# Expert units loaded in two halves, the input half released by the up step

## The reference, cut to what matters

```python
def block(tb):                                   # 128 tokens
    s = jnp.einsum('thsk,hsnk->thsn', qr, sub_keys)
    top_s, top_i = lax.top_k(s, PEER_TOPK)
    ...
    gate = jax.nn.softmax(best_s, axis=-1)       # 8 heads x 16 experts a token
    act = gelu(jnp.einsum('td,thkd->thk', tb, expert_u[idx]))
    w = gate * act
    return jnp.einsum('thk,thkd->td', w, expert_v[idx])
```

## Time and profile before

| | |
|---|---|
| median of 3 runs | 3339.25 us (3337.97 to 3349.36) |
| the profiled execution, its own time | 3346.74 us |
| its span in the profile | 3344.9 us |
| TensorE busy, share of the span | 2946.0 us, 88% |
| VectorE busy | 2258.0 us, 68% |
| ScalarE busy | 1341.0 us, 40% |
| GpSimd busy | 202.2 us, 6% |
| moved by transfers | 645.03 MB, 193 GB/s on average |
| expert stage of layer 0 | about 965 to 2040 us of the span |
| expert stage of layer 1 | about 2635 to 3313 us of the span |

### The profile page before, as it was taken

How to read it: one execution, slowest core, us unless ns; L and a number is a source line. 1 busy time by engine, 2 the same in 40 slices (tenths; PEclk the granted TensorE clock), 3 DMA queues, 4 the chain that set the end, 5 groups by cost and what they waited for, 6 DMA issues and landing times.

```text
span 3344.9 us, 48195 instructions
## 1 busy us (share of the span) xinstructions
PE 2946.0 (88%) x17119; PEld 2417.9 (72%) x17119; DVE 2258.0 (68%) x4420; ACT 1341.0 (40%) x2255; POOL 202.2 (6%) x238
## 2 busy tenths in 40 slices
PE   6999899754789999999999998978772899999998
PEld 2855454543679898898999996767662788888886
DVE  1337241669987777777777774275459988888886
ACT  2122220211974444444444443122213855655553
POOL 0000000000001111111111110000000000000000
PEclk7899999866999999999999998989996999999998
DMA  9122212524237877878777773223230378777774
GB/s 373 58 83 79 85 38 88 203 87 177 109 142 255 285 265 275 271 267 281 255 253 254 251 251 113 76 95 114 98 139 26 116 298 299 303 300 287 292 287 188
DMA packets 127609, 645.03 MB, mean 193 GB/s; under 512 B 11520, under 2 KB 45472, under 8 KB 55584
## 3 DMA queue, kind: packets, MB, share of 16 engines
q1 hardware_dynamic: 98656, 434.13, 35.7%
q0 software_dynamic: 28864, 209.76, 17.5%
HBM read 624.02 MB, written 19.79 MB: 192 GB/s over the span
## 4 chain that ended last, share of the span: by engine, by line
PE 66%; DVE 16%; DMA 8%; ACT 7%; issue 3%; DVEq 0%; ACTq 0%; SPq 0%
PE ps L611 65%; DMA ring<-in_experts 6%; ACT hot L1336 2%; DMA ring<-in_w_mod 1%; DVE hot L1827 1%; DVE gbuf L1850 1%; ACT ehi L1349 1%; DVE topi L1744 1%; DVE topi L1752 1%; DVE hot L1822 1%; DVE sc L1746 1%; ACT gateB L1322 1%; DVE top L1741 1%; DVE top L1749 1%; DVE hot L1825 0%
## 5 line engine op out<-in xcount | busy, mean ns | idle before, releaser
L611 PE MATMUL ps<-h2a,ehi 128*128 128x384 f32 x2048 | 522.4, 336 | 3.5 <-DVE elo L1837 3.5
L1837 DVE TENSOR_TENSOR elo<-ring,ehi 128x1024 fp32r<-128x1024 f32 x256 | 312.3, 1221 | 125.0 <-ACT ehi L1349 124.6
L611 PEld LDWEIGHTS ps<-h2a,ehi 128*128 128x128 f32 x2048 | 372.8, 188 | 15.2 <-DVE elo L1837 5.2
L1349 ACT ACTIVATE ehi<-ring 128x1024 fp32r<-128x1024 f32 x256 | 270.6, 1058 | 259.8 <-DMA ring<-in_experts 259.5
L1872 DVE TENSOR_TENSOR elo<-ring,ehi 128x1024 fp32r<-128x1024 f32 x256 | 312.9, 1222 | 68.0 <-ACT ehi L1375 67.9
L1375 ACT ACTIVATE ehi<-ring 128x1024 fp32r<-128x1024 f32 x256 | 269.9, 1054 | 205.9 <-PE ps L611 205.4
L611 PE MATMUL ps<-h2b,ehi 128*128 128x192 f32 x2048 | 349.1, 274 | 2.1 <-DVE elo L1837 2.1
L611 PE MATMUL ps<-h2a,elo 128*128 128x384 f32 x1024 | 343.7, 336 | 0.0
L611 PEld LDWEIGHTS ps<-h2b,ehi 128*128 128x128 f32 x2048 | 320.8, 192 | 23.9 <-DVE elo L1837 6.6
L611 PE MATMUL ps<-hT,ring 128*128 128x512 f32 (+1 forms) x896 | 307.7, 502 | 0.0
L594 POOL DMA_INDIRECT gbuf<-in_expert_rows,gidx x192 | 185.5, 966 | 1834.8 <-DVE yg L1860 1700.0
(11 more groups left out here) (320 smaller groups left out, 4556.4 us busy)
## 6 DMA issues: line engine op xcount, KB each, us to landing
ring<-in_experts SPq DMA_DIRECT2D x256, 1024.0 KB, 4.8
ring<-in_w_mod SPq DMA_DIRECT2D x48, 1024.0 KB, 7.7
ring<-in_w_side SPq DMA_DIRECT2D x24, 1024.0 KB, 4.9
ring<-in_w_front SPq DMA_DIRECT2D x12, 1024.0 KB, 4.9
ring<-in_w_merge SPq DMA_DIRECT2D x16, 768.0 KB, 4.3
ring<-in_w_q SPq DMA_DIRECT2D x12, 1024.0 KB, 5.0
gate_scratch<-spill SPq DMA_DIRECT2D x48, 256.0 KB, 2.0
gateA<-gate_scratch SPq DMA_DIRECT2D x4, 3072.0 KB, 20.3
```

Source lines behind the costliest of these rows:

```text
L611: return pe.matmul(out, w, x, start=start, stop=stop, **k)
L1349: act.activation(ehi[:, k % 2, :], ring[:, (u + k) % RING, 0:DM], ACT.Copy).then_inc(uhi_ready, 1)
L1837: v.tensor_tensor(elo[:, r, 0:DM], ring[:, r, 0:DM], ehi[:, k % 2, :].bitcast(F32), ALU.subtract).then_inc(ulo_ready, 1)
```

## The change

Every expert unit is loaded by two transfers of 512 KB: columns 0 to 1023 by `load_in`, columns 1024 to 2047 by `load_out`. `load_in` of unit n waits for `a_ready` of up(n-4), `load_out` of unit n for `used` of down(n-4). The halves have semaphores of their own: `u_in` (new) for the input half, for which `u_high` now waits, and `unit_in` for the output half, for which `v_high` now waits besides `used`. On the queue the input half of unit n+1 stands ahead of the output half of unit n. The rest of the kernel stays. Without its file names and blank lines:

```diff
@@ -354,6 +354,7 @@
         const_in = sem("const_in")
         unit_in = [sem(f"unit_in{s}") for s in range(RING)]
+        u_in = [sem(f"u_in{s}") for s in range(RING)]
         keys_in = sem("keys_in")
         mcst_in = sem("mcst_in")
@@ -477,6 +478,48 @@
                     for k in range(RING):
                         load(u + head + k, src[bass.ds(i * RING + (head + k), 1)].rearrange("o p n -> (o p) n"), i, RING)
+            def load_in(l, k, i=None):
+                e, n = BASE[("experts", l, 0)] + k, units_before(("experts", l, 0)) + k - RING
+                if i is not None:
+                    sp.wait_ge(a_ready, i * RING + (n + 1))
+                    src = a["experts"][l, bass.ds(i * RING + k, 1)].rearrange("o p n -> (o p) n")
+                else:
+                    if k >= RING:
+                        sp.wait_ge(a_ready, n + 1)
+                    else:
+                        sp.wait_ge(used[e % RING], e // RING)
+                    src = a["experts"][l, k]
+                sp.dma_start(ring[:, e % RING, 0:DM], src[:, 0:DM]).then_inc(u_in[e % RING], 16)
+            def load_out(l, k, i=None):
+                e = BASE[("experts", l, 0)] + k
+                sp.wait_ge(used[e % RING], e // RING if i is None else i + e // RING)
+                src = a["experts"][l, k] if i is None else a["experts"][l, bass.ds(i * RING + k, 1)].rearrange("o p n -> (o p) n")
+                sp.dma_start(ring[:, e % RING, DM:2 * DM], src[:, DM:2 * DM]).then_inc(unit_in[e % RING], 16)
+            def experts_begin(l):
+                for k in range(RING):
+                    load_in(l, k)
+                for k in range(RING):
+                    load_out(l, k)
+            def experts_turns(l, first, n):
+                with sp.Fori(0, n) as i:
+                    for k in range(RING):
+                        load_in(l, first + k + 1, i)
+                        load_out(l, first + k, i)
+            def experts_end(l):
+                for k in range(NK - RING, NK):
+                    if k + 1 < NK:
+                        load_in(l, k + 1)
+                    load_out(l, k)
             for st in stages:
                 kind, l, h = st
                 u = BASE[st]
@@ -528,9 +571,8 @@
                     if half is not None:
                         stream(u + WQ_UNITS, a["w_mod"][l + 1, MOD_UNITS // 2 * half:MOD_UNITS // 2 * (half + 1)], MOD_UNITS // 2)
                 elif kind == "gates" and l < DEPTH - 1:
-                    gb, e = groups_before(st), BASE[("experts", l, 0)]
-                    for k in range(RING):
-                        load(e + k, a["experts"][l, k])
+                    gb = groups_before(st)
+                    experts_begin(l)
                     with sp.Fori(0, dense_tokens(l) // 16) as i:
                         for b in range(2):
@@ -540,24 +582,22 @@
                 elif kind == "experts" and l < DEPTH - 1:
                     back = a["gate_scratch"].rearrange("m p n t -> p m n t")
-                    def turns(first, n):
-                        with sp.Fori(0, n) as i:
-                            for k in range(RING):
-                                load(u + first + k, a["experts"][l, bass.ds(i * RING + (first + k), 1)].rearrange(
-                                    "o p n -> (o p) n"), i, RING)
+                    load_in(l, RING)
                     for b in range(NEAR // BACK):
-                        turns(RING + BACK * b, BACK // RING)
+                        experts_turns(l, RING + BACK * b, BACK // RING)
                         s_ = slice(BACK * b, BACK * (b + 1))
                         for parity in range(2):
                             sp.wait_ge(spill_out[parity], 8 * spills_before(st))
                         count(sp, w_ready, units_before(st) + BACK * (b + 1))
                         sp.dma_start(gateA[:, :, s_, :], back[:, :, s_, :]).then_inc(gate_back, 16)
-                    turns(RING + NEAR, (NK - NEAR) // RING - 1)
+                    experts_turns(l, RING + NEAR, (NK - NEAR) // RING - 2)
+                    experts_end(l)
                 elif kind == "experts":
-                    stream(u, a["experts"][l], NK)
+                    experts_begin(l)
+                    load_in(l, RING)
+                    experts_turns(l, RING, NK // RING - 2)
+                    experts_end(l)
                 elif kind == "final":
                     sp.wait_ge(fin_ready, KD)
                     sp.dma_start(a["out"], fout[:, :, :]).then_inc(stored, 16)
@@ -1343,7 +1383,7 @@
                     actT = peer_tiles(l)[3]
                     def u_high(k, i):
-                        arrived(act, u + k, i, RING)
+                        act.wait_ge(u_in[(u + k) % RING], i * 16 + 16 * ((ub + k) // RING + 1))
                         if k >= 2 or not isinstance(i, int):
                             act.wait_ge(a_ready, i * RING + (ub + k - 1))
                         act.activation(ehi[:, k % 2, :], ring[:, (u + k) % RING, 0:DM], ACT.Copy).then_inc(uhi_ready, 1)
@@ -1371,6 +1411,7 @@
                     def step(k, i, ahead):
+                        arrived(act, u + k, i, RING)
                         unit_used(act, u + k - 2, i, RING)
                         act.activation(ehi[:, 2 + k % 2, :], ring[:, (u + k) % RING, DM:2 * DM], ACT.Copy
                                        ).then_inc(vhi_ready, 1)
```

## The result

| | before | changed |
|---|---|---|
| median, runs side by side on one chip | 3342.99 us (3337.97 to 3349.36, 4 runs) | 3298.4 us (3297.42 to 3302.09, 4 runs) |
| ratio of the two | 1 | 0.9863, interval 0.9849 to 0.9877 |
| span of the profiled execution | 3344.9 us | 3295.6 us |
| expert stage of layer 0, first up step to last down step | 1071.3 us | 1063.7 us |
| expert stage of layer 1, likewise | 677.7 us | 638.9 us |

The change makes the kernel 44.6 us faster by the medians. The prediction said 44, and 3295 us for the median, from a median of before that lay 3.7 us lower (3339.25 against 3342.99). The last two lines are from the starts and ends of the matmuls in the traces. The stages give 38.8 and 7.6 us; the other 2.9 us of the spans' difference lie outside them, where nothing was changed.

What follows compares the result with a forecast made beforehand. TensorE's matmuls were taken as the bound, with stalls in layer 1 from late expert loads. 37 us (layer 1) plus 7 us (layer 0) make 44; 3339.25 less 44 gives 3295 us, range 3290 to 3303.

Steps and rivals of the forecast that it cites:

- Step 1: Layer 1's expert stage: input halves asked for earlier end ScalarE's waits and TensorE's stalls; 37 us won, between 20 and 41.
- The clock's part: Layer 1's expert stage: the granted clock drops to 0.50 behind long stalls; 6 us taken as won back.
- the prediction's 33.0 us: Layer 1's expert stage: TensorE's weight loads waited 26.4 us for wB and 6.6 us for elo, the most to win there.
- The 3 us kept for the edge: Layer 1, edge of each four-unit turn: the vector engine's margin is thin, about 0.6 us, so 3 us of stalls stay.
- The first rival: Turn's edge takes over: vector engine or gathered row 1.2 us later at 31 edges, 19 us lost, 3314 us; chance 0.09.
- Steps 2 and 3: Expert stages: ScalarE's later wait for the output half, and 512 loads instead of 256 on the sync queue, each cost nothing.
- Step 4: Layer 0, four gate returns: less data ahead lands unit 20's input half 2.3 us sooner; 7 us won, between 3 and 8.4.
- The rule about sizes: Expert loads: at least 1 MiB per DMA is asked for; halves in series would add some 180 us over 128 units.
- Loads not the cause: Expert stage: stalls aren't the loads', or halves don't come sooner; 0 to 10 us won, 3329 to 3339; chance 0.07.
- transfers the bound: Layer 1's expert stage: smaller transfers carry only 280 GB/s where 308 are needed, 22 us more there, 3354 us; chance 0.05.

Runs made afterwards that it cites:

- series of releases: Four half-transfer kernels with the input half released at down n-4, up n-3, down n-5, up n-4 (the change): 3329.44, 3310.57, 3296.51, 3298.4 us.
- halves alone: Against the changed kernel, the input half is released with the whole unit's event, down step of unit n-4, output half right behind it: 3329.44 us, ratio 0.9967.
- the wide product: Changed kernel plus an unread 128x1024 vector-engine product, without a wait of its own, at each of 31 turn edges in layer 1: 3318.32 us, ratio 0.9915.
- quarters: Against the changed kernel, each half is loaded in two transfers of 256 KB, four a unit: 3298.77 us, ratio 0.9839.
- The run that makes the prediction's mechanism true: Against the changed kernel, the queue order puts unit 20's input half behind the return of gates in layer 0: 3303.72 us, ratio 0.9856.

## Why the prediction was right, and where it wasn't

**Step 1, layer 1: right in mechanism and size.** 37 us were forecast (39 to 41, less 3 kept), 38.8 measured, close to the 39 by waits and clock. What the forecast needed was a landing within 10.6 us; the halves land in 4.0 to 7.3 us, median 5.4, not quite the 4 to 6 given. The series of releases shows the cause: the loss falls with the release, at one and the same size. The prediction had not seen that halves alone, without any earlier release, win 22 us of it; this is worth knowing, since it means that the gain isn't one thing.

The clock's part can be estimated from the traces. The kernel before was at the lower level of 1.2 GHz in four stretches of this stage, each right behind a long stall: the two of the earlier trace rows and, with length, busy PE, granted clock, DMA share and GB/s,

```profile
3193.00:3196.00 3.00, 3.00 (x9) 0.51 0.01 5
3238.00:3240.50 2.50, 2.50 (x11) 0.50 0.14 16
```

The four are some 14 us together. At half speed they give back about 7 us, an estimate, where 6 were forecast; in the changed kernel the granted clock is 1.00 over the stage. TensorE's own idle time was 24.4 us. The rest of the 38.8 us, between 7 and 8, shows neither as idle time nor as clock. The run with the wide product has such a part too: 18.0 us lost at a clock of 1.00, of which TensorE stood idle for 11.0. So the prediction's 33.0 us, the waits of the weight loads, was the right row to add up, and TensorE's idle time would have been too little.

**The 3 us kept for the edge: wrong, nothing is lost there.** The margin was put at 0.57 to 0.76 us. Measured with extra products it is 0.5 us: a little under the forecast, and enough, since the product that uses it up must take longer than that. It can't be read from the timelines of the vector engine and TensorE at an undisturbed edge of the changed kernel, unit 56 again, answering to the earlier trace rows:

```profile
2907.41 0.43 DVE L1933 TENSOR_TENSOR wB<-actB,wB 128x64 fp32r<-128x64 f32 x2
...
2909.78 0.64 PE L651 MATMUL ps<-ehi,wB 128*128 128x512 f32 x2
```

The weights are done at 2907.84 (2907.41 plus 0.43), 1.94 us before TensorE uses them. That is not the margin: it is a lead that the vector engine has built up. A further 1.14 us in each turn ate it within two turns in the run with the wide product, and then every edge cost 0.6 us. The first rival (edge, 3314 us) put such a case: some 1.2 us more at each of 31 edges, 19 us lost. The wide product made it: 18.0 us lost, 3318.32 us.

**Steps 2 and 3: right.** The output half's wait doesn't show in layer 1; in layer 0 it is 1.1 us in all, 0.3 at most, at the four returns. The queue takes twice the issues without a loss, and four times (quarters). Moved bytes are as before, and so is the busy time of the engines, but for TensorE's, which fell from 2946.0 to 2926.7 us with the stalls.

**Step 4, layer 0: right size, wrong mechanism, so the 7 us are luck.** 7 us forecast, 7.6 measured. The prediction had unit 20's input half behind the return, landing 2.3 us sooner since it and what stands ahead of it are half as large. In fact it stands ahead, by one place, because each turn loads the input half of the *next* unit, and it is asked for 4.6 us before the return. What stands behind is unit 21's, which has a whole unit (8.3 us) more until it is used. ScalarE does wait for it, up to 2.3 us in each of the four places, and the vector engine up to 1.6 us for ScalarE, but TensorE for neither:

```profile
ACT ehi L1389 <- DMA ring<-in_experts: 8.4, 4, 2.3
```

The run that makes the prediction's mechanism true keeps 5.8 us of the 7.6 as a loss, and its profiled span is 3303.1 us where the change has 3295.6. So with the place on the queue that the prediction had in mind, its step 4 would have been worth 1.8 us. The mistake was in reading the listing of the order: the input half behind the return was taken for the one of the unit just due.

**The rule about sizes.** The prediction set a rule of the Trainium skill, page "DMA: Bandwidth & Descriptors", section "Rules for kernel authors" (at least 1 MiB per DMA), against the change, with some 180 us more if halves ran in series. They don't: halves are issued every 2.5 us and land in 5.4, so one goes while others are on their way. Here the trace doesn't bear the rule out in time, down to 256 KB. It agrees in direction: at the same 316 GB/s the DMA engines are busy for 0.88 of the time with halves and 0.92 with quarters. What the rule asks about, the highest rate, was not tried, since TensorE bounds this stage.

**The rivals.** "Loads not the cause" and "transfers the bound" are out: stage and rate both moved as forecast, and a rate of 320 GB/s is over the 308 that were needed. Not tried was a rate at which the transfers would bound the stage.

## What to carry to other kernels

Where a buffer holds two things that are used up at different times, let each be refilled at its own event: it buys lead without memory. Splitting and releasing are two gains: here the halves alone won 22 of the 39 us in layer 1, since fewer landed late, and the earlier release the other 17. Before adding a place on a queue, find out which *unit* stands on either side of each large transfer on it, and whether what you put ahead of that transfer holds it back. Lead seen in a profile is not throughput to spare; to price what an engine can still take on, add a little work and read what each turn loses.

## What the runs showed of the hardware that was not expected

Behind the 3 MB return of gates the next issue on the same queue is held: it took 6.19 us in the kernel before, where an issue takes 0.33, 11.58 in the changed one, and 9.69 to 13.21 us in the variants, each at the first return. There it ended 13.9 to 16.5 us after the return's own issue, whenever it began (13.6 to 18.5 us over all four returns of all the runs). So a transfer right behind this one starts hardly sooner for being released sooner; in the one pair of runs that varies it, it came 3.0 us sooner with the return itself issued 3.1 us sooner. That this is the queue filling up with the return's pieces (128x48x128, so rows of 512 bytes) is likely, but was only argued; no run changed the return's shape.
